# Gate tiles of a state space block moved from the input product into the recurrence, and decay rows over 128 partitions

## The reference

```
z, xBC, dt = split(h @ ssm_w_in)        # 2048 gate columns, 4096 conv columns, 32 step sizes
xBC = silu(causal_conv4(xBC))           # 16 tiles x, 8 tiles B, 8 tiles C of 128 columns
dt = softplus(dt + dt_bias); A = -exp(a_log)
# 8 groups of 4 heads, chunks of 128 tokens:
y = within_chunk(decay, B, C, x * dt) + exp(cs) * (C @ carried_state) + d_skip * x
y = y * silu(z)                         # the gate
y = y * rsqrt(mean(y*y in its group) + 1e-5) * ssm_norm
out = y @ ssm_w_out
```

## Time and profile before

| | |
|---|---|
| median of 3 runs | 3415.45 us |
| lowest and highest | 3414.63, 3415.87 us |
| span of the profiled execution, first to last instruction | 3412.0 us |
| the median above that span | 3.4 us |
| TensorE busy (matmuls) | 3234.2 us, 95% |
| VectorE, ScalarE, GpSimd busy | 1571.2, 894.9, 1659.6 us |
| input product of the state space block, last tile | ends at about 2026 us |
| first matmul of the output product | starts at about 2204 us |

### The profile page before, as it was taken

The page is one execution under the profiler, slowest core; times in us unless marked ns, Lnnn a source line. Parts: engine busy times, 40 slices in busy tenths (PEclk is TensorE's granted clock), DMA queues, the critical chain, the costliest instruction groups (busy, mean ns, idle before and its releaser), DMA issues.

```text
span 3412.0 us, 41810 instructions
## 1 busy us (share of the span) xinstructions
PE 3234.2 (95%) x15832; PEld 2637.7 (77%) x15832; DVE 1571.2 (46%) x2390; ACT 894.9 (26%) x1630; POOL 1659.6 (49%) x880
## 2 busy tenths in 40 slices
PE   7998799999999998999989999899999998899998
PEld 3888777888899755788867876688888787778887
DVE  5877638732232763211035557615541365645521
ACT  3122222111253353111022224422221213632210
POOL 1540034666787403566646640166666563056664
PEclk9998899999999999999999988899999999999999
DMA  5530014642454101223222320023232222022331
GB/s 217 193 127 7 1 63 176 234 154 94 132 183 157 62 1 56 74 98 106 91 64 87 98 68 1 19 93 98 93 111 88 88 91 70 1 80 93 98 105 67
DMA packets 84545, 319.21 MB, mean 94 GB/s; under 512 B 9200, under 2 KB 10864, under 8 KB 83376
## 3 DMA queue, kind: packets, MB, share of 16 engines
q1 hardware_dynamic: 84400, 317.20, 27.6%
HBM read 315.06 MB, written 2.10 MB: 93 GB/s over the span
## 4 chain that ended last, share of the span: by engine, by line
PE 84%; DVE 8%; ACT 4%; issue 2%; POOL 2%; DMA 1%; SPq 0%; DVEq 0%; POOLq 0%; ACTq 0%
PE two L332 16%; PE two L334 16%; PE two L333 16%; PE two L459 7%; PE two L460 7%; PE two L461 7%; PE two L2024 1%; PE two L2004 1%; ACT d_p L2266 1%; PE two L2549 1%; PE two L1452 1%; PE two L1455 1%; PE two L2589 1%; PE two L2013 1%; DMA ada_n<-ada0n 1%
## 5 line engine op out<-in xcount | busy, mean ns | idle before, releaser
L332 PE MATMUL two<-h_hi,w_hi 128*128 128x512 f32 x2280 | 903.4, 396 | 8.6 <-POOL w_lo L283 3.5
L334 PE MATMUL two<-h_hi,w_lo 128*128 128x512 f32 x2280 | 894.2, 392 | 0.0
L333 PE MATMUL two<-h_lo,w_hi 128*128 128x512 f32 x2184 | 853.2, 391 | 0.0
L283 POOL TENSOR_TENSOR w_lo<-w_raw,w_hi 128x1024 fp32r<-128x1024 f32 x315 | 772.0, 2452 | 34.8 <-ACT w_hi L356 10.2
L281 POOL TENSOR_SCALAR w_hi<-w_raw 128x1024 fp32r<-128x1024 f32 x295 | 316.1, 1072 | 799.8 <-issue 385.4
L332 PEld LDWEIGHTS two<-h_hi,w_hi 128*128 128x128 f32 x2280 | 428.9, 188 | 105.2 <-issue 7.5
L334 PEld LDWEIGHTS two<-h_hi,w_lo 128*128 128x128 f32 x2280 | 428.5, 188 | 96.2
L438 POOL TENSOR_SCALAR w_hi<-w_raw 128x1408 fp32r<-128x1408 f32 (+1 forms) x106 | 133.9, 1263 | 731.5 <-PE two L461 491.3
L333 PEld LDWEIGHTS two<-h_lo,w_hi 128*128 128x128 f32 x2184 | 410.6, 188 | 90.6 <-issue 1.4
L440 POOL TENSOR_TENSOR w_lo<-w_raw,w_hi 128x1408 fp32r<-128x1408 f32 (+1 forms) x112 | 339.3, 3031 | 10.5 <-ACT w_hi L496 1.6
L459 PE MATMUL two<-hid_hi,w_hi 128*128 128x512 f32 x704 | 276.2, 392 | 0.0
(11 more groups left out here) (486 smaller groups left out, 5300.4 us busy)
## 6 DMA issues: line engine op xcount, KB each, us to landing
w_raw<-w_f0u SPq DMA_DIRECT2D x88, 512.0 KB, 3.5
row_raw<-ada SPq DMA_DIRECT2D x48, 512.0 KB, 5.3
w_raw<-w_ssm SPq DMA_DIRECT2D x48, 512.0 KB, 3.4
w_raw<-w_f0d SPq DMA_DIRECT2D x32, 704.0 KB, 4.1
w_raw<-w_f1u SPq DMA_DIRECT2D x44, 512.0 KB, 3.4
w_raw<-w_f2u SPq DMA_DIRECT2D x44, 512.0 KB, 3.5
w_raw<-w_f3u SPq DMA_DIRECT2D x44, 512.0 KB, 3.4
ada_raw<-ada SPq DMA_DIRECT2D x32, 512.0 KB, 3.7
```

The source lines that it names most:

```text
L283: nc.gpsimd.tensor_tensor(lo[:, 0:self.kt], w_raw[j][:, 0:self.kt], hi[:, 0:self.kt].bitcast(f32), ALU.subtract).then_inc(split_done, 1)
L332: nc.tensor.matmul(dst, w_h[:, k], hi, start=kk == 0, stop=False)
L333: nc.tensor.matmul(dst, w_h[:, k], lo, start=False, stop=False)
L334: last = nc.tensor.matmul(dst, w_l[:, k], hi, start=False, stop=kk == self.parts * self.kt - 1)
```

## The change

In words:

- The 16 gate tiles leave the input product, which is now `Gemm(w_ssm, 32, ...)` over conv tiles alone (the weights' order in memory is changed to suit). `Ssd` loads, splits and multiplies them: `gate_product(n)` issues the next n steps of 128 in all, 8 ahead of the first group, then 16 in each of groups 0 to 6 and 8 in group 7, in pieces between the group's other steps. All go into bank 7.
- The carried state's two tiles therefore share bank 6, the second waiting for VectorE's multiply of the first.
- A gate is no longer ScalarE's Silu. VectorE scales it (`z_scaled`), ScalarE makes the sigmoid by Exp, Ln, Exp (`sigmoid`), VectorE multiplies the two, and the last output multiply reads that.
- `DtSide` stays in the product, which has no gate tiles now; its pieces are put behind other tiles: VectorE's behind (1,2), (2,0), (2,2) and (3,1) instead of (1,1), (1,2), (1,3) and (2,2); ScalarE's Exp piece behind (3,0), TensorE's transposes behind (4,1).
- `sel`, `s_pair`, `cs_two` and `ec_two` have 128 partitions instead of 64, the added half zero, so that `row` and `spread` contract over 128.
- Buffers are laid out anew; the output product uses banks 0, 4, 5, 7 instead of 4, 5, 7, 3 and has other gates; the scratch for GpSimd's own DMAs is 1024 bytes.

```diff
@@ SsmConv.dve
                     nc.vector.tensor_tensor(g.out(n), g.out(n), rstd[:], ALU.mult).then_inc(self.scaled[0], 1)
-                    if a < 4:
-                        g.side.dve(dve, i, n)
-                        continue
-                    t = 4 * i + n - 16
+                    t = 4 * i + n
...
+                    g.side.dve(dve, i, n)
@@ DtSide
-                if (i, n) == (1, 1):
+                if (i, n) == (1, 2):
                     dve.wait_ge(*upto(self.dt_act, 1))
...
-                if (i, n) == (1, 2):
+                if (i, n) == (2, 0):
                     for c in (7, 5, 3, 1):
...
-                if (i, n) == (1, 3):
+                if (i, n) == (2, 2):
...
@@ Ssd.pool
+                def split(m):
+                    n = self.chunk0 + m
+                    raw, hi, lo = w_raw[n % RAW][:, 0:ND], w_hi[n % SPL][:, 0:ND], w_lo[n % SPL][:, 0:ND]
+                    pool.wait_ge(raw_ready[n % RAW], 16 * (n // RAW + 1))
+                    pool.wait_ge(chunk_done, n + 1)
+                    nc.gpsimd.tensor_scalar(hi, raw, 1.0, 1.0, ALU.mult, ALU.mult).then_inc(hi_done, 1)
+                    pool.wait_ge(hi_done, n + 1)
+                    nc.gpsimd.tensor_tensor(lo, raw, hi.bitcast(f32), ALU.subtract).then_inc(split_done, 1)
@@ Ssd.pe
-                    nc.tensor.matmul(ps[3][:], sel[:, h:h + 1].to_broadcast([2 * NSH, P]), cs_two[:], start=True, stop=False)
+                    nc.tensor.matmul(ps[3][:], sel[:, h:h + 1].to_broadcast([P, P]), cs_two[:], start=True, stop=False)
...
+                def gate_product(steps):
+                    for _ in range(steps):
+                        m, k = next(z_steps)
+                        n = self.chunk0 + m
+                        if k == 0:
+                            pe.wait_ge(split_done, RAW + n + 1)
+                            if m:
+                                pe.wait_ge(mm_free, NBANK + self.tile0 + m)
+                        nc.tensor.matmul(ps[7][:], w_hi[n % SPL][:, k], h_hi[:, k], start=k == 0, stop=False)
+                        nc.tensor.matmul(ps[7][:], w_hi[n % SPL][:, k], h_lo[:, k], start=False, stop=False)
+                        last = nc.tensor.matmul(ps[7][:], w_lo[n % SPL][:, k], h_hi[:, k], start=False, stop=k == ND - 1)
+                        if k == ND - 1:
+                            last.then_inc(chunk_done, 1)
...
+                    gate_product(1)
                     spread(g, 0)
                     within(g, 0)
+                    gate_product(1)
                     spread(g, 1)
                     within(g, 1)
-                    if g + 1 < NG:
+                    gate_product(1)
+                    if more:
                         turned_x(g + 1, 0)
                         turned_x(g + 1, 1)
+                    gate_product(2)
                     if g:
                         total(g - 1)
+                    gate_product(3)
                     row(g + 1, 0)
                     within(g, 2)
                     row(g + 1, 1)
                     within(g, 3)
...
+                    if more:
+                        gate_product(2)
+                    carried(g, 0)
+                    if more:
+                        gate_product(2)
+                    carried(g, 1)
+                    if more:
+                        gate_product(1)
                     row(g + 1, 2)
-                    if g + 1 < NG:
+                    if more:
+                        gate_product(2)
                         head(g + 1)
+                        gate_product(1)
                     row(g + 1, 3)
@@ Ssd.act
+                    astep(nc.scalar.activation(z_sig[m % 2][:], z_gate[m % 4][:], ACT.Exp, scale=-1.0))
+                    astep(nc.scalar.activation(z_sig[m % 2][:], z_sig[m % 2][:], ACT.Ln, bias=ones[:, 0:1]))
+                    nc.scalar.activation(z_sig[m % 2][:], z_sig[m % 2][:], ACT.Exp, scale=-1.0).then_inc(self.z_sig[0], 1)
@@ Ssd.dve
+                def z_scaled(m):
+                    if m == 2 * NG:
+                        return
+                    dve.wait_ge(chunk_done, SPL + self.chunk0 + m + 1)
+                    nc.vector.tensor_tensor(z_gate[m % 4][:], ps[7][:], rstd[:], ALU.mult).then_inc(mm_free, 1)
...
                     for k in range(4):
+                        if k == 2:
+                            for m in (2 * g, 2 * g + 1):
+                                dve.wait_ge(*upto(self.z_sig, m + 1))
+                                nc.vector.tensor_tensor(z_gate[m % 4][:], z_gate[m % 4][:], z_sig[m % 2][:], ALU.mult).then_inc(self.z_gated[0], 1)
```

More of the change, by code:

```diff
@@ L450, in pe @@
                         pe.wait_ge(*self.tile_read(t - len(self.banks)))
-                    elif part == 0 and t == 3 and self.bank_gate:
+                    elif part == 0 and t == self.bank_gate_at and self.bank_gate:
                         pe.wait_ge(*self.bank_gate)
@@ L571, in build, with __init__ @@
         class AddGainTail(AddTail):
-            def __init__(self, gain):
-                self.sum = SquareSum(between=(1, 2))
+            def __init__(self, gain, acc=None, bufs=None):
+                self.sum = SquareSum(acc=acc, bufs=bufs, between=(1, 2))
                 self.rstd_ready = cnt.take("rstd_ready", 1)
@@ L2304, in act @@
                     nc.scalar.activation(dst, c_acc[n % 2][:], ACT.Silu, bias=vec[:, bass.ds(VEC["conv_b"][0] + t, 1)]).then_inc(self.out[0], 1)
+                    g.side.act(act, i, n)
             def dve(self, g, dve, i, a):
@@ new lines, in build @@
+        s_prev = arena("s_prev", [P, 4, 256], 52 * K)
+        s_e = [arena(f"s_e{i}", [P, TL], (56 + 2 * i) * K) for i in range(2)]
+        s_out = [arena(f"s_out{i}", [P, TL], (60 + 2 * i) * K) for i in range(2)]
+        z_gate = [arena(f"z_gate{i}", [P, TL], (132 + 2 * i) * K) for i in range(4)]
+        z_sig = [arena(f"z_sig{i}", [P, TL], (140 + 2 * i) * K) for i in range(2)]
+        g_rstd = arena("g_rstd", [P, TL], 144 * K)
+        p_acc = arena("p_acc", [P, TL], 32 * K)
+        p_sq = [arena(f"p_sq{i}", [P, TL], (34 + 2 * i) * K) for i in range(2)]
@@ L2342, in build @@
-        d_t = [arena(f"d_t{i}", [NSH, TL], (102 + 2 * i) * K) for i in range(3)]
+        sel = arena("sel", [P, NSH], 131 * K, f32r)
+        cs_two = at("cs_two", [P, TL], o_xc + 4 * K, f32r)
+        ec_two = at("ec_two", [P, TL], o_xc + 6 * K, f32r)
+        d_dt = arena("d_dt", [NSH, TL], 112 * K)
+        d_cs = arena("d_cs", [NSH, TL], 114 * K)
+        d_ec = arena("d_ec", [NSH, TL], 116 * K)
+        d_t = [arena(f"d_t{i}", [NSH, TL], (118 + 2 * i) * K) for i in range(3)]
         mask_r = at("mask_r", [P, P], made["mods0"][0] + 512, f32r)
@@ L2473, in __init__ @@
                 self.product, self.conv, self.dt = product, conv, dt
+                self.w_z, self.chunk0, self.tile0 = product.w, progress["chunk"], progress["tile"]
+                progress["chunk"] += 2 * NG
+                progress["tile"] += 2 * NG
+                self.z_sig, self.z_gated = cnt.take("z_sig_ready", 2 * NG), cnt.take("z_gated", 2 * NG)
                 n = NG
@@ L2552, in pe, with carried @@
                 free = lambda n: (mm_free, NBANK + self.product.tile0 + n)
+                z_steps = iter([(m, k) for m in range(2 * NG) for k in range(ND)])
+                def gate_product(steps):
+                    for _ in range(steps):
+                        m, k = next(z_steps)
+                        n = self.chunk0 + m
+                        if k == 0:
[7 more added lines that the diff above has]
+                            last.then_inc(chunk_done, 1)
+                def carried(g, t):
+                    if t == 0:
+                        pe.wait_ge(*upto(self.prev, 4 * g + 4))
+                    else:
+                        pe.wait_ge(*upto(self.y_step, 8 * g + 1))
+                    for c in range(4):
+                        last = nc.tensor.matmul(ps[6][:, c * P:(c + 1) * P], s_prev[:, c, t * P:(t + 1) * P], tiles(g)[2][:, c * CH:(c + 1) * CH], start=True, stop=True)
+                    last.then_inc(self.yo[0], 1)
+                gate_product(8)
                 pe.wait_ge(*upto(self.conv, 16))
@@ L2566, in pe @@
                 for g in range(NG):
-                    _, b, cc = tiles(g)
+                    more = g + 1 < NG
                     pe.wait_ge(*upto(self.b_ready, g + 1))
@@ L2585, in pe @@
                     within(g, 3)
-                    pe.wait_ge(*upto(self.prev, 4 * g + 4))
-                    for t in range(2):
-                        for c in range(4):
-                            last = nc.tensor.matmul(ps[6 + t][:, c * P:(c + 1) * P], s_prev[:, c, t * P:(t + 1) * P], cc[:, c * CH:(c + 1) * CH], start=True, stop=True)
-                        last.then_inc(self.yo[0], 1)
+                    if more:
[6 more added lines that the diff above has]
+                        gate_product(1)
                     row(g + 1, 2)
-                    if g + 1 < NG:
```

(11 more changed lines are left out.)

98 lines of the change are left out of this document (55 added, 43 removed).

## The result

| | before | after |
|---|---|---|
| median of 5 runs | 3415.87 us | 3394.56 us |
| lowest and highest | 3414.63, 3420.85 us | 3386.87, 3395.77 us |
| ratio, 95% interval | | 0.9936 [0.9922, 0.9951] |
| profiled execution: span, time | 3412.0 us | 3392.8, 3394.57 us |

What follows compares the result with a forecast made beforehand. TensorE, busy 95% of the span, bounds the kernel; recurrence groups are loops of short waits, partly at 1.2 GHz. Terms -75.5 + 1 + 38.3 + 10 + 6.4 - 1.5 + 9 = -12.3 us gave median 3403, range 3386 to 3422.

Steps and rivals of the forecast that it cites:

- A: The forecast itself: time within 7 us of 3403, its own range 3396 to 3410; chance 0.42.
- group 0's +10: First recurrence group, with no norm of a predecessor: 26.0 us against 15.96, so +10.
- B: Rival: covers hold better, no collision on VectorE's leg, no junction cost, side stops of 8 to 12; about 3386; chance 0.23.
- What comes back in the product: Input product: DtSide between conv tiles causes TensorE stops of 17.9 us; 12.3 of the 87.8 us saved come back.
- Prologue: Ahead of group 0: eight steps cover the 3.42 us wait and keep the clock up; +1 net, bounds -2 and +3.
- Groups 1 to 6: Middle recurrence groups: 16.2 us of TensorE work plus 11.0 of gate steps, 27.1 each; +38.3 in all.
- rows, junctions and collisions: Recurrence corrections: 5.6 us saved by 128 rows, 4.1 lost at shape junctions, net -1.5; GpSimd collisions +9.
- Group 7: Last recurrence group with 8 gate steps, partly hidden in its idle time: +6.4, bounds 3 and 7.5.
- Collisions: GpSimd's splits delay VectorE's leg in the groups: 1.3 us a group, 7 times, +9; bounds 0 and 3.2 a group.
- C: Rival: longer product stops because every DtSide piece meets GpSimd again, 22 rather than 12.3 us; 3413; chance 0.17.
- E: Rival: VectorE bounds the groups, all 4.5 us in its leg, 13 us more than A: 3416; chance 0.08.
- Rival D: Slower: the new groups keep the 0.84 granted clock, 3.1 us more TensorE time each, 22 in seven: 3425; chance 0.10.

Runs made afterwards that it cites:

- Experiment 2: The changed kernel with the DtSide pieces, ScalarE's Exp piece and the transposes behind their old tiles; median 3392.92 us, ratio 0.9941 to the kernel before.
- experiment 3: The changed kernel with GpSimd's split of a group's first chunk held until VectorE has the second weight; median 3383.82 us, ratio 0.9913 to the kernel before.
- experiment 1: The changed kernel with row and spread contracting over 64 partitions again; median 3396.44 us, ratio 0.9955 to the kernel before.
- Experiment 8: The changed kernel with group 7's eight gate steps moved among the prologue's row steps; median 3390.55 us, ratio 0.9919 to the kernel before.
- experiment 5: The kernel before with only the row steps over 128 partitions, spread still over 64; one execution, 3405.74 us.
- experiment 7: The changed kernel with a group's 16 gate steps in two blocks of eight instead of ten pieces; one execution, 3410.37 us.

## Why the prediction was right, and where it was off

The mechanism was mostly A, and its main term, 27.1 us for a group at full clock, was met by 27.03; group 0's +10 was met too. The time of 3394.56 us lies 8 under the 3403 forecast, inside the whole range and 1.4 below A's own. It is as far from B's 3386. The gain is nearly twice the forecast, and in the stretch, free of the first layer's 7.0 us, it is twice (25.3 for 12.3): that the time came so near A is in part the luck of a late start. By its steps:

- **What comes back in the product**: mis-sized. Forecast 12.3 net, measured 6.7 (87.8 less 81.1). Its "VectorE 4.2 us" a tile was read from the late tiles and is 3.69 among the early ones, so the stops were 6.5 us. The forecast's 17.9 were to take in all by which the last tile is late against `1784.5 + 27 x 5.49`; that is 12.3 (1952.09 less the offset of 7.0). So 5.8 of it are no stops, and TensorE's timeline has them. After the stops ten and nine matmuls start some 0.4 us apart (1828.14 to 1832.13, 1855.63 to 1859.38) where 0.23 is the pace, 3.4 us of low clock; the transposes (1873.58 to 1875.41) take 1.4 us beyond that pace; and the first tiles run at 0.233 a matmul, before the change too, some 0.6 in all. With the stops these make 11.9. Experiment 2 shows that the new places of the pieces are worth 5.5 us in the product and 3.8 in the stretch.
- **Prologue**: forecast +1, measured -2.1, beyond the lower bound by a tenth. The eight steps cover the wait of 3.42, as said, and give back more than that in clock: the prologue's granted clock is 0.94, where it was 0.61 before (2026.10 to 2043.15).
- **Groups 1 to 6**: the base was right and the correction wrong. Of the 7.5 us added for rows, junctions and collisions, most in these groups, nothing remained. Collisions cost 1.0 us a group, as experiment 3 shows (forecast 1.3). Against them stood 1.2 us of saved drains, six of 0.2, since `spread` drains too; I had counted four. The junctions with `within`, 0.6 a group, cost 0.1 at most: with 64 rows TensorE's work is 27.22 us (experiment 1), the forecast's 27.1 without any junction. The Trainium skill, "TensorEngine Tiling", Key Properties, says that a change of tiling mode drains the engine; the trace agrees for 64 to 128 rows (0.43 against 0.24), and for the 64-column matmuls in kind: `spread` to `within` is 0.32 (2049.70 to 2050.02) for a pace of 0.23, too little to show in a group's length.
- **Group 7**: too small, 9.9 for 6.4, outside its bounds of 3 and 7.5. I counted TensorE's steps and half hid them; VectorE bounds this group, and all that it does more comes before the last norm. TensorE waits 1.0, 3.0 and 6.4 us there and runs at 0.80. Experiment 8 gives the steps' part, 5.8 us. The wait of 3.0 is one that the forecast had covered by two gate steps: the carried state's second step waits for bank 6, and group 7 has no steps there. A second collision made it longer, with GpSimd's split for the output product (timelines of VectorE, GpSimd and TensorE):

```profile
2169.81 3.69 DVE L2762 TENSOR_TENSOR ssm_lo<-s_out,ssm_hi 128x512 fp32r<-128x512 f32 x2
...
2170.29 2.66 POOL L441 TENSOR_TENSOR w_lo<-w_raw,w_hi 128x1024 fp32r<-128x1024 f32 x1
...
2174.15 2.08 PE L2604 MATMUL two<-zx,s_prev 128*128 128x128 f32 x8 [3.02 <-DVE s_e L2820]
```

The two subtractions of 3.69 us take 1.35 in experiment 8, where that split had already been made.

- **Collisions**: right in kind and nearly in size. The place is one weight later than in the forecast's leg: it is the second weight that TensorE waits for. The tenths that the forecast gave to semaphores are not seen at this place: that weight ends at 2053.20, and TensorE starts at 2053.26.
- **Rival B**, 3386, is nearer in its product's stops than A, and right that the junctions cost next to nothing; it wanted no collision, and there was one. **C** and **E** fall: stops of 6.5 us, and groups of 27.0.
- **Rival D** named the largest force of this case, but asked only whether the low clock would stay. That clock costs the kernel before 15.3 us, and either part of the change removes it by itself: 128 rows alone make the stretch 424.60, the gate steps alone 418.96, both 414.65 of 439.94. So the effects don't add: the second to come gets only its own part (10 us for the move, 4.3 for the rows). I had reckoned with full clock in the new groups and put it down to the waits that vanish; that the rows alone would give it, 15.3 us, stood nowhere in my sum.

What holds the clock is narrowed, not settled. The Trainium skill, "TensorE: Matmul & The Clock Gate", A second HAM failure mode, ties an alternating clock to frequent short idles. By it the groups with 3.1 us idle of 18.2 (experiment 5) should be worse than before's; they ran at 1.00, so these traces don't bear the rule out as it stands. With steps of 64 rows and no gate steps the clock falls to 0.84; with gate steps between, 64 rows do no harm (experiment 1); with 128 rows and the gate steps in blocks (experiment 7) four groups fell to 0.94 and two stayed at 1.00, all six with 3.4 us idle. Neither the row count nor the idle time alone explains all four. Idle time at a fixed mix of matmuls, and the places of the waits at a fixed amount, were not tested.

## What to carry to other kernels

Read the granted clock of each stage before you count instructions: a loop at 0.84 offers more than the instructions that a change saves in it, and the cheapest cure (zero rows to fill the contraction) may be worth as much as the large one. Work moved into a loop of short waits costs less only by the waits that it covers, so it has to stand in each of them: against the 18.2 us of a full-clock group, 11.0 us of gate steps cost 8.8 a group in ten pieces and all 11.0 in two blocks, which with the clock that fell made 20 us here. When a filler engine shares a port with a critical one, move the filler's start behind the critical instruction, not its work away.
